# First norm with another order of transfers, weight splits and low parts and with products without use; attention scores of the odd layer ahead of half a gate panel

## What is computed

```python
u = _rms_norm(h, norm_mix_g[l])      # x * rsqrt(mean(x*x) + EPS) * g
proj = u @ w_in[l]
```

```python
u = x @ od_w_in[i]
gq, gk, gv, g_low, gr, c_q, c_kv, k_r = split_cols(u, ODD_SPLITS)
yc = gla_mixer(...)     # rms_norm(o, g_norm) * silu(gr)
yd = mla_mixer(...)     # softmax(q k^T * scale, causal) v
y = jnp.concatenate([yc, yd], axis=-1) @ od_w_out[i]
```

## Time and profile before

| | before |
|---|---|
| device time, median of 3 runs | 2102.76 us (2102.47 to 2104.9) |
| device time of the profiled execution | 2102.12 us |
| span of that execution in the trace | 2100.2 us |
| mean granted clock of TensorE | 0.986 |
| busy share PE / DVE / ACT / POOL | 96% / 45% / 35% / 17% |

### The profile page before, as it was taken

The page is one execution under the profiler, slowest core; times in us unless marked ns, Lnnn a source line. Parts: engine busy times, 40 slices in busy tenths (PEclk is TensorE's granted clock), DMA queues, the critical chain, the costliest instruction groups (busy, mean ns, idle before and its releaser), DMA issues.

```text
span 2100.2 us, 27114 instructions
## 1 busy us (share of the span) xinstructions
PE 2025.5 (96%) x11486; PEld 1197.9 (57%) x11486; DVE 946.0 (45%) x1209; ACT 727.0 (35%) x1121; POOL 351.2 (17%) x358
## 2 busy tenths in 40 slices
PE   7999989989999999999999999999999899999997
PEld 5643435575676444588557544447865566444466
DVE  5654467564544332225565422222655654222224
ACT  5432221144534332123453322221553634222213
POOL 1011200021012220005002521200340025121100
PEclk9999989999999999999999999999999999999999
DMA  6211110022322222322212233332121122332221
GB/s 234 81 61 40 61 40 21 20 101 101 103 98 81 100 100 100 103 100 99 81 61 81 81 103 102 111 105 102 61 81 61 41 81 67 103 110 102 101 101 41
DMA packets 28180, 179.65 MB, mean 86 GB/s; under 512 B 2913, under 2 KB 7137, under 8 KB 7137
## 3 DMA queue, kind: packets, MB, share of 16 engines
q1 hardware_dynamic: 27264, 170.93, 23.6%
q10 hardware_dynamic: 512, 4.94, 0.7%
q0 software_dynamic: 288, 2.10, 0.3%
HBM read 175.86 MB, written 2.10 MB: 85 GB/s over the span
## 4 chain that ended last, share of the span: by engine, by line
PE 87%; DVE 9%; ACT 3%; issue 1%; DMA 1%; POOL 0%; ACTq 0%; DVEq 0%; SPq 0%
PE psum_a L374 24%; PE psum_a L375 24%; PE psum_a L376 24%; PE psum_b L507 2%; PE psum_a L687 2%; DVE X L1771 1%; PE psum_a L629 1%; PE psum_den L627 1%; DVE RINV L1745 1%; DVE W_PARTS L1751 1%; PE psum_a L698 1%; ACT W_PARTS L1196 1%; PE psum_b L607 1%; DVE ARENA L1771 1%; PE psum_b L1021 1%
## 5 line engine op out<-in xcount | busy, mean ns | idle before, releaser
L1751 DVE SCALAR_TENSOR_TENSOR W_PARTS<-W,W_PARTS 128x2048 f16<-128x2048 f32 x145 | 332.6, 2297 | 614.6 <-ACT W_PARTS L1196 614.5
L374 PE MATMUL psum_a<-U,W_PARTS 128*128 128x512 f16 (+1 forms) x1304 | 489.6, 375 | 8.5 <-POOL U L2513 3.9
L375 PE MATMUL psum_a<-U,W_PARTS 128*128 128x512 f16 (+1 forms) x1304 | 489.6, 375 | 0.0
L376 PE MATMUL psum_a<-U,W_PARTS 128*128 128x512 f16 (+1 forms) x1304 | 489.4, 375 | 0.0
L1196 ACT ACTIVATE W_PARTS<-W 128x2048 f16<-128x2048 f32 x145 | 275.7, 1905 | 491.4 <-PE psum_a L376 491.4
L374 PE MATMUL psum_a<-ARENA,W_PARTS 128*128 128x256 f16 (+2 forms) x956 | 295.6, 309 | 3.7 <-DVE W_PARTS L1751 3.0
L375 PE MATMUL psum_a<-ARENA,W_PARTS 128*128 128x256 f16 (+2 forms) x956 | 295.5, 309 | 0.0
L376 PE MATMUL psum_a<-ARENA,W_PARTS 128*128 128x256 f16 (+2 forms) x956 | 295.5, 309 | 0.0
L374 PEld LDWEIGHTS psum_a<-U,W_PARTS 128*128 128x128 f16 x1304 | 128.2, 98 | 158.7 <-DVE W_PARTS L1751 9.3
L376 PEld LDWEIGHTS psum_a<-U,W_PARTS 128*128 128x128 f16 x1304 | 128.2, 98 | 148.1 <-issue 1.6
L375 PEld LDWEIGHTS psum_a<-U,W_PARTS 128*128 128x128 f16 x1304 | 128.1, 98 | 147.5 <-issue 4.0
(11 more groups left out here) (302 smaller groups left out, 2705.9 us busy)
## 6 DMA issues: line engine op xcount, KB each, us to landing
W<-weights SPq DMA_DIRECT2D x159, 1024.0 KB, 4.8
CON<-const ACTq DMA_DIRECT2D x1, 3071.5 KB, 11.4
X<-x_in SPq DMA_DIRECT2D x2, 1024.0 KB, 7.3
U<-dft POOLq DMA_DIRECT2D x1, 1024.0 KB, 5.4
ARENA<-dft POOLq DMA_DIRECT2D x1, 1024.0 KB, 5.3
ARENA<-mem_in ACTq DMA_DIRECT2D x1, 1024.0 KB, 4.7
y_out<-U SPq DMA_DIRECT2D x2, 512.0 KB, 3.0
y_out<-U SPq DMA_DIRECT2D x4, 256.0 KB, 2.2
```

Of the source, the lines that this page charges most:

```text
L374: nc.tensor.matmul(out, left(0), right(0), start=first, stop=False)
L375: nc.tensor.matmul(out, left(0), right(1), start=False, stop=False)
L376: return nc.tensor.matmul(out, left(1), right(0), start=False, stop=last)
L1751: nc.vector.scalar_tensor_tensor(out=home[:, 1, :], in0=W[g % 2][:, :], scalar=W_SCALE, in1=home[:, 0, :], op0=ALU.mult, op1=ALU.subtract) ...
```

## The change

At the start, SP issues half 0 of the input as four transfers of two tiles each, waits for the second of them, and then issues panel 0, half 1 of the input, and panel 1. ACT loads the square-root table first, and squares the tiles of half 0 as their transfers land. After the root of half 0 it splits panel 0, writes the high parts of half 0, splits panel 1, and only then squares half 1; it issues the tables after the root of half 1. DVE makes the low parts of half 0 itself, right after panel 0's low part, and panel 1's ahead of the reciprocal of half 1; GpSimd's loop is gone. PE gets 10 products of the ones with themselves ahead of the first sum and 32 behind it (`keep_busy`, fp16, 512 columns, into `psum_den`, read by nobody), and does the sum of half 1 after panel 0 with half 0.

In the odd layer, `row_scores(MLA, 2)` and `head_sums("gla")` move into the hook ahead of gr's second tile, `head_roots("gla")` moves ahead of `row_turns(MLA, 2)`, and ACT and DVE have their steps in an order to match: `gr_copy(3)` after `row_copies(MLA, 1)`, and the split of oo's second panel, `used(("gr", 1))`, after `row_copies(MLA, 2)` on ACT and after `row_norm(MLA, 3)` on DVE.

```diff
--- before.py
+++ after.py
@@ -540,9 +540,16 @@
                 return lambda kt: pe.wait_ge(sem(f"low_{name}"), 8 * (n_pieces(name) - 1) + kt + 1)
 
 
+            def keep_busy(n):
+
+                data = ones_wide.bitcast(F16)[:, 0:T]
+                for _ in range(n):
+                    nc.tensor.matmul(psum_den[:, :], data[:, 0:P], data, start=True, stop=True)
+
             pe.wait_ge(sem("ones_set"), 1)
-            for half in range(2):
-                norm_sum("mix", half)
+            keep_busy(10)
+            norm_sum("mix", 0)
+            keep_busy(32)
             first_in, first_banks = [], {}
             for half in range(2):
                 for n, name in enumerate(("gate", ("in", 6))):
@@ -561,6 +568,8 @@
                                            lambda l: U16[:, l, kt, HALVES[half]], kt == 0, kt == KT - 1)
                             if half and kt == KT - 1:
                                 last.then_inc(A.done, 1)
+                    if half + n == 0:
+                        norm_sum("mix", 1)
                     released[g] = A.done, A.n
 
             in_panel = []
@@ -1118,14 +1127,14 @@
                 gla_outputs(1)
                 row_scores(MLA, 1, score_mla)
                 row_turns(MLA, 0)
+                row_scores(MLA, 2, score_mla)
+                head_sums("gla", 4, lambda h: KS[:, h, :], one_row, G)
 
             project_panel("gr", 1, U16, after=gr1_after)
-            row_scores(MLA, 2, score_mla)
-            head_sums("gla", 4, lambda h: KS[:, h, :], one_row, G)
             row_turns(MLA, 1)
             row_scores(MLA, 3, score_mla)
+            head_roots("gla", 4, RINV[0:64, :], row_back)
             row_turns(MLA, 2)
-            head_roots("gla", 4, RINV[0:64, :], row_back)
             for tt in range(4):
                 pe.wait_ge(A.freed_sem(("mv", tt)), A.freed_at(("mv", tt)))
             for b in range(3):
@@ -1337,17 +1346,18 @@
 
 
             act.wait_ge(sem("eps_set"), 2)
-            for half in range(2):
-                act.wait_ge(sem(f"x_landed{half}"), 16)
-                squares("mix", half, in_x)
-                if half:
-                    split(0)
-                root("mix", half)
-            act.dma_start(CON[:, n_ones:], const[:, n_ones:]).then_inc(sem("tables_landed"), 16)
-            act.dma_start(SMALL[0:64, :], small_w).then_inc(sem("small_landed"), 16)
+            root_table()
+            squares("mix", 0, in_x, lambda kt: act.wait_ge(sem(f"x_landed0_{kt // 2}"), 16))
+            root("mix", 0)
+            split(0)
             for kt in range(KT):
                 high_tile("mix", 0, kt, in_qk, U16)
             split(1)
+            act.wait_ge(sem("x_landed1"), 16)
+            squares("mix", 1, in_x)
+            root("mix", 1)
+            act.dma_start(CON[:, n_ones:], const[:, n_ones:]).then_inc(sem("tables_landed"), 16)
+            act.dma_start(SMALL[0:64, :], small_w).then_inc(sem("small_landed"), 16)
             for kt in range(KT):
                 high_tile("mix", 1, kt, in_qk, U16)
             split(2)
@@ -1713,13 +1723,13 @@
                 nc.scalar.activation(KS[:, h, :], OGL[:, h, :], ACT.Square).then_inc(sem("gla_squared"), 1)
             row_exps(MLA, 1)
             row_copies(MLA, 0)
-            gr_copy(3)
-            used(("gr", 1))
             root_rows("gla", ROOT[0:64, :], P, G)
             row_exps(MLA, 2)
             row_copies(MLA, 1)
+            gr_copy(3)
             row_exps(MLA, 3)
             row_copies(MLA, 2)
+            used(("gr", 1))
             row_copies(MLA, 3)
             for h in range(4):
                 high(sem("gla_mixed"), h + 1, MIX16[:, 0, h, :], OGL[:, h, :], "gla_high")
@@ -1970,14 +1980,16 @@
 
             taps = PAR[:, PARAM["conv_w0"][0]:PARAM["conv_w2"][0] + PARAM["conv_w2"][1]]
             nc.vector.tensor_scalar(taps, taps, DESCALE, None, ALU.mult).then_inc(sem("taps_scaled"), 1)
-            inverse("mix", 0)
-            gain_tiles("mix", 0, in_x, in_qk, "norm_mix")
-            split(0)
-            inverse("mix", 1)
-            gain_tiles("mix", 1, in_x, in_qk, "norm_mix")
-            split(1)
-            for kt in range(KT):
-                low("high_mix", 8 + kt + 1, U16[:, 1, kt, HALVES[1]], in_qk(kt, 1), U16[:, 0, kt, HALVES[1]], "low_mix1")
+            for half in range(2):
+                inverse("mix", half)
+                gain_tiles("mix", half, in_x, in_qk, "norm_mix")
+                if half == 0:
+                    split(0)
+                for kt in range(KT):
+                    low("high_mix", 8 * half + kt + 1, U16[:, 1, kt, HALVES[half]], in_qk(kt, half), U16[:, 0, kt, HALVES[half]],
+                        f"low_mix{half}")
+                if half == 0:
+                    split(1)
             split(2)
             dve.wait_ge(sem("taps_scaled"), 1)
 
@@ -2507,10 +2519,6 @@
                         pool.wait_ge(sem(f"high_{name}"), 8 * half + kt + 1)
                         out, high_part = parts16[:, 1, kt, HALVES[half]], parts16[:, 0, kt, HALVES[half]]
                         nc.gpsimd.tensor_tensor(out, src(kt, half), high_part, ALU.subtract).then_inc(sem(f"low_{name}"), 1)
-
-            for kt in range(KT):
-                pool.wait_ge(sem("high_mix"), kt + 1)
-                nc.gpsimd.tensor_tensor(U16[:, 1, kt, HALVES[0]], in_qk(kt, 0), U16[:, 0, kt, HALVES[0]], ALU.subtract).then_inc(sem("low_mix0"), 1)
 
 
             pool.wait_ge(sem("tables_landed"), 16)
@@ -2611,9 +2619,11 @@
                 src = weights[g] if i is None else weights[i * 2 + g]
                 sp.dma_start(W[g % 2][:, :], src).then_inc(landed[g % 2], 16)
 
-            for half in range(2):
-                sp.dma_start(X[:, :, HALVES[half]], x_in[:, :, HALVES[half]]).then_inc(sem(f"x_landed{half}"), 16)
+            for n in range(4):
+                sp.dma_start(X[:, 2 * n:2 * n + 2, HALVES[0]], x_in[:, 2 * n:2 * n + 2, HALVES[0]]).then_inc(sem(f"x_landed0_{n}"), 16)
+            sp.wait_ge(sem("x_landed0_1"), 16)
             load(0)
+            sp.dma_start(X[:, :, HALVES[1]], x_in[:, :, HALVES[1]]).then_inc(sem("x_landed1"), 16)
             load(1)
             pairs = (N_PANELS - 2) // 2
             with sp.Fori(0, pairs) as i:
```

## The result

| | before | changed |
|---|---|---|
| device time, median of 5 runs each | 2102.47 us (2099.67 to 2104.9) | 2089.37 us (2086.66 to 2092.09) |
| profiled execution, its span | 2102.12, 2100.2 us | 2087.47, 2085.7 us |
| granted clock, mean | 0.986 | 0.990 |

The ratio of the times is 0.9935, with a 95% interval of 0.9918 to 0.9952: the changed kernel is 0.65% faster. The direction came out as forecast, the size did not. That the median fell just outside the range and not just inside is the luck of five runs, two of which lie in it; the gain of 10.0 us that I forecast was too small in any case, as the experiments show. Three executions among all that follow, of 2301.87, 5134 and 10529 us, were slow ones and are left out everywhere.

A forecast was written before the change was run, and what follows sets the result against it. TensorE (PE), with 87% of the chain, was taken as the bound, its idle and half-clock places as the gain. 2102.1-4.7 (start)-5.3 (odd layer)=2092.1, with the runs' median 0.6 higher: 2092.7 us, range 2089.8 to 2096.8.

The forecast's parts named there:

- (a): Start: input half 0 comes as four 256 KB transfers, the fourth landing between 4.9 and 6.8 us, taken as 6.0.
- (c): Start: ten unused products bring PE to full clock between 5.0 and 6.1 us, so the first sum ends at 9.6.
- (e): Start: the 32 unused products fill 9.6 to 16.5 us, leave 1.3 us idle and cost nothing.
- (g) to (i): Start: half 1's sum costs 3.6 us in PE's stream; after its chain half 1 starts at 32.5, not 37.2.
- R1: Rival at the start: all 16 sum products run at 1.2 GHz, the ten buying nothing; 2095.6 us, chance 0.12.
- R2: Rival at the start: the input quarters land in series, all in at 9.5 us; 2093.8 us, chance 0.10.
- R4: Rival at the start: unused products never raise the clock and hold PE, half 1 12 us late; 2109.5 us, chance 0.03.
- (j) to (m): Odd layer: with scores and DVE steps reordered, the wait ahead of row_turns(2) ends at 1661.3, only 1 us earlier.
- (n): Odd layer: head_roots fills the gap, 1.3 us idle keeps the clock, and row_turns(2) takes half of its 2.75 us.
- (o): Odd layer: DVE's 3.32 us scaling of four GLA heads is next late; om_block ends at 1669.5, not 1674.8.
- R3: Rival in the odd layer: the gap only changes cause, an extra table load; gain there 3.3, 2094.7 us, chance 0.08.
- R5: Rival for both edits: no difference within 0.2%, waits only move to a later feed; chance 0.05.

The follow-up runs named there:

- odd_only: The kernel before with only the odd layer's edit, the start as before: mean 2096.40 us, ratio 0.9966.
- no_products: The changed kernel without its 10 and 32 products nobody reads: mean 2091.17 us, +1.4 ±0.8 against the changed kernel.
- ten_only: The changed kernel without the 32 products behind the first sum, the ten kept: mean 2089.41 us, -0.4 ±0.8 against the changed kernel.
- lows_pool: The changed kernel with half 0's low parts back on GpSimd: mean 2092.07 us, +2.3 ±0.9 against the changed kernel.
- gap_filled: The kernel before with 24 products nobody reads in PE's gap ahead of row_turns(MLA, 2): 2100.25 us, 3.2 ±0.6 below before.
- before_again: The kernel before, unedited, profiled and run once more: median 2101.77 us, ratio 0.9999.
- start_only: The kernel before with only the edit at the start, the odd layer as before: mean 2099.74 us, ratio 0.998.

## Why the prediction was right, and where it was wrong

**The start held, step by step.** (a) I took 6.0 for the last quarter; the sum ran without a wait from 5.57 and (c) ended at about 9.5, where I had 9.6. (d) The first product came at 17.81, forecast 17.8. (e) The 32 products fitted into the 8.2 us, with a gap of 1.37 that kept the clock. (g) to (i) Half 1 came at 32.64, forecast 32.5; 4.63 us gained, forecast 4.7. Over all profiles half 1 starts at 37.6 with the old start and at 32.2 with the whole new one, 5.4 us. R1 and R2 did not happen: the sum was fast, and the quarters did not come in series. R4 did not either: the sum behind the ten products goes at 0.22 us an instruction, and the 32 end before the first product is due.

**The odd layer's gain held, with one step wrong.** (j) to (m) The wait's end came where it was due, with 1.20 us left idle against a forecast of 1.3. Step (n), "1.3 us, less than the gap at 32.02 that kept the clock", failed in this execution: the turns took 2.6 us and not 1.4. It cost only 0.7 us, since (o) DVE's scaling of the heads, 2.72 us where I had 3.32, ended at 1654.5 anyway, and the turns at 1654.6. The stretch shrank by 5.2 us, forecast 5.3. The clock fell at this gap in three profiles (odd stretch 44.40 to 44.42) and kept up in four (43.68 to 43.71, `odd_only`, `no_products`, `ten_only`, `lows_pool`), so one gap of before could not decide it. R3 did not happen, and R5 is ruled out by the 13.7 ±0.8 us.

**Two terms failed, and both are TensorE's clock.** The first is the size of the odd term. It took what the clock costs behind the old gap from one profile: half of `row_turns(2)`, 1.4 us, and little in `head_roots`, 1.6 in all by `gap_filled`'s. Over runs it is 3.2 ±0.6, and 6.8 ±1.1 with the new start. The odd edit is worth 7.1 ±0.5 us alone and 2099.74-2089.78=10.0 ±0.8 on top of the start edit, where I had 5.3: too small in either order.

The second is a term that I put at nothing. That "what is won before 37.2 stays won" gives the start edit no effect on the clock later on. It has two. It takes 1.9 us out of the piece ahead of `row_scores(0)`, and it makes the half clock behind the old gap cost more, by 4.1 us in the profiles and 3.6 ±1.3 in the runs, which counts only as long as that gap is there. Alone the start edit gains 3.7 ±0.6 us; on top of the odd edit it gains 2096.40-2089.78=6.6 ±0.8, and with the gap filled 7.3 ±1.1, where I had 4.7. In profiles that is 4.6 to 5.4 at the start plus the 1.9, so 6.5 to 7.3. Both orders give the same sum: 3.7+10.0 or 7.1+6.6 is 13.7, and I had 10.0. That the start step came out at 4.63 against 4.7 was right; that it would be all the start edit does was not.

The range failed with these. Its upper ends were worked out with one execution's clock, and the allowance beside them came from three runs 2.4 us apart, where 70 lie 9.3 apart. The profiled pair's 14.6 us is near the runs' 13.7 partly by luck, as 2.8 of it is the chance part of the middle.

Open are why the half clock behind the old gap lasts longer with the start edit, why the one near 1621 us goes with it, where the gap's 3.2 us of the runs lie when two profiles show 1.6, and what the 42 products and the quarters are worth each.

## What to carry to other kernels

A gap on TensorE costs its length and, behind it, a stretch at half clock whose length one profile does not tell; where the engine is the bound, fill a gap that can't be closed, first with work that is due anyway (`head_roots`, 4.0 us of the odd stretch), else with products nobody reads. Judge the worth of an edit by stretches between two points that both kernels pass, and the stretches that no edit touches by several profiles: here one of them moved 4.75 us, as much as an edit, of which 2.8 were chance and 1.9 came with the start edit in every profile. Cut such a stretch in pieces before calling it chance: its mean over the profiles was the same and hid the piece. Run two edits apart and together, as their gains need not add up. Where the first consumer can start on a part, try the first input in parts and ahead of all else, even against the bandwidth.

## What the runs showed of the hardware that was not expected

- After the same 5.7 us gap, TensorE's half clock (1.2 GHz) lasted through `row_turns(2)` in `before_again` (2.8 us, then `head_roots` in 4.03) and through 12 us of unbroken matmuls in `start_only`.
- After the same gap of 1.20 us the clock fell in three profiles and kept up in four. The Trainium skill (TensorE: Matmul & The Clock Gate, "What's actually happening") calls the number of slow products after a start "run-variable". The runs here show the like at a gap in the middle of a kernel, where it even varies whether the clock falls.
- The same 8615 matmuls between two fixed points took 1559.0 to 1564.7 us over 14 profiles, but the last 600 or so of them 100.8 in each with the old start and 98.9 in each with the new one.
- Of the 70 runs of before 26 took 2104.9 us or more, with a mean clock of 0.983 or 0.984 where it is known, and 43 took 2102.8 or less, with 0.986 or 0.988; `gap_filled` had none above 2102.81 in 12.
